# Reordering splits, copies, value products and scores inside the attention stage of a hybrid inference step

## The chip, the cores and the metric

The kernel runs on one core of a Trainium2 chip. The metric is the device time of one execution in microseconds (us); the time before is the median of three runs. A matmul works on TensorE (PE in the profile, with its weight loads as PEld), element-wise work on VectorE (DVE) and ScalarE (ACT), masks on GpSimd (POOL), and SyncE (SP) starts most transfers. Each engine takes its instructions in the order in which they were written, and waits on semaphores hold up all that is written behind them on that engine.

## What is computed

Two layers of a streaming encoder for 512 prompt tokens and 64 new tokens with 512 cached rows. Layer 0 has 8 stick-breaking heads and 8 forgetting-attention (fox) heads; layer 1 is latent attention (mla); both are followed by a mixture of experts. Cut to what the change touches, layer 0 computes for every head (head size 64):

```
z = h @ w_in                                   # q, k, v of all heads
# fox head
s = q @ k.T * 64**-0.5;  p = softmax(where(pos_k <= pos_q, s + decay, -1e30));  o = p @ v
# stick-breaking head
z = q @ k.T * 64**-0.5
log_beta = where(before, log_sigmoid(z), -1e30);  log_rest = where(before, log_sigmoid(-z), 0)
a = exp(log_beta + reverse_cumsum(log_rest) - log_rest);  o = a @ v
```

## The kernel before

Heads are taken two at a time, as eight pairs: pairs 0 to 3 stick-breaking ("sb"), pairs 4 to 7 fox. `attend` is used for layer 0 (`mla` false) and for layer 1 (`mla` true); the change keeps the order of layer 1. Each pair p is cut into ten units u (5 blocks of query rows times 2 heads). Per unit, PE computes scores (L626), ACT and DVE turn them into probabilities (`shares` L801, `cut` L1065 on POOL and `stick` L969 for sb; `decay` L1051 on POOL, `logits` L957, `exponent` L811 and `even` L982 for fox), PE transposes them (`turn` L654), ACT copies the transposed ones out of PSUM (`turn_out` L819), and after both heads of a block PE multiplies them with v (`values` L665) and DVE copies the result to `mix` (`finish` L991).

Beside the attention of pair p, PE computes the projections of pair p+1, each half of q, k and v as 24 matmuls (`project_ab`, L574; a product and its two correction products, L203 to L205). The units after which they stand are in `AB_AFTER` (L384): q0 ahead of unit 0, q1 after 0, k0 after 1, k1 after 3, the transposes of k (kt) after 4, v0 after 5, v1 after 7, the transposes of v (vt) after 8. ACT and DVE copy each out of PSUM (`copy_out`, L743 and L891), and PE's next projection into the same bank waits for that copy (`banks_free`, L569).

Further work stands between these copies:

- `split(p, par, n)` (L789, L947) splits the weights of q, k or v (n = 0, 1, 2) into a high part on ACT (L193) and a low part on DVE (L197). `splits` (L711) puts w_v of p+1 after unit 1, w_q of p+2 after unit 4, w_k of p+2 after unit 8. SP reloads the weights once they are split (`load_w`, L491).
- Two ACT copies double q for both halves of the partitions, right after q1's copy (L779); two ACT copies and two DVE subtractions split k, right after k1's copy (L784, L938).
- `split_past` splits the cached keys, after unit 0's copies on ACT and after unit 1's on DVE. SP loads the next ones when DVE's part is done (`load_past`, L501).

The order on PE in one pair (L680) is: scores of units 0 to 3; then per unit the turn, the value product of an earlier block (at u = 3, 5, 7, 9), the scores of unit u+4, the projections; at the end the value product of the last block. On each engine the order is exactly as written out in its own `pair` function; there is no planner.

Of the kernel before, what the change touches and what calls it, by code (L numbers as in the profile page):

```python
# [388 lines left out]
def attend(k, mla, m, gates=None):  # L389
# [6 lines left out]
    with ExitStack() as c:  # L396
# [83 lines left out]

        def steps_after(after, u):
            return [name for name in after if after[name] == u]

        with nc.Block() as block:
# [83 lines left out]
            def _(pe):  # L568
# [111 lines left out]
                def pair(p, par, kind, more):  # L680
# [30 lines left out]
            def splits(split, p, par, u):  # L711
# [11 lines left out]
            def first_copies(split, copy_out, gates_part):  # L723
# [5 lines left out]
                for step in copied:  # L729
                    copy_out(0, 0, step)  # L730
                    if not mla:
                        {"q1": lambda: split(0, 0, 2), "k1": lambda: split(1, 1, 0), "v1": lambda: split(1, 1, 1)}.get(step, lambda: None)()
# [3 lines left out]
            def _(act):  # L736
# [6 lines left out]
                def copy_out(p, par, step):  # L743
# [35 lines left out]
                    if step == "q1":  # L779
                        hi = q_hi[par]  # L780
                        hold(act, passed, (s["proj_act"], n), (s["q_hi_done"], 2 * p + 2))
                        copy(r32(hi[0][HD:P, :]), hi[0][0:HD, :])
                        copy(r32(hi[1][0:HD, :]), hi[1][HD:P, :]).then_inc(s["q_twice"], 1)
                    if step == "k1":  # L784
                        hold(act, passed, (s["proj_dve"], n))
                        copy(r32(k_both[par][0][0:HD, 0:T]), kT[0:HD, :]).then_inc(s["k_hi_done"], 1)
                        copy(r32(k_both[par][1][HD:P, 0:T]), kT[HD:P, :]).then_inc(s["k_hi_done"], 1)
# [41 lines left out]
                def pair(p, par, kind, more):  # L829
# [1508 lines left out]
```

## Time and profile before

| | |
|---|---|
| median of three runs | 1471.54 us (1470.74 to 1478.39) |
| the profiled execution | 1466.02 us |
| its span in the profile | 1464.2 us |
| PE busy, all of the span | 1184.6 us (81%) |
| DVE, ACT, POOL busy | 690.8, 427.9, 246.4 us |
| layer 0's attention (scores of pair 0 to values of pair 7) | 46.2 to 363.7 us |
| mixture of experts 0, attention 1, mixture 1 | behind it, to the end |

The page of the profile gives shares over the whole span, which is a mean over four stages with different limits. The stage in question is read with three views of the trace: busy time by stretches, waits, and the timeline (start us, duration us, engine, line, operation, output<-input with shapes, count, and in brackets the idle time of that engine just before and what ended it). The granted clock is TensorE's clock as a share of 2.4 GHz, so 0.5 is 1.2 GHz.

### The profile page before, as it was taken

The numbers are of one execution on the slowest core, as the hardware profiler recorded it, in microseconds if no ns is written. First come the engines' busy times: TensorE is split into PE (matmuls) and PEld (weight loads), VectorE is DVE, ScalarE is ACT, GpSimd is POOL, SyncE is SP. The second block draws the span as 40 slices with busy tenths as digits, with TensorE's granted clock in tenths as the row PEclk, the third lists the DMA queues.
The fourth block names the chain that finished last, engine by engine and source line by source line (L and its number), as shares of the span: only waits on it lengthen the run. The fifth ranks groups of instructions, "written<-read, shape, count | busy, mean of one in ns | idle before, by whom it ended". The sixth has DMA issues, their size and how long they took to land. (4 is left out here: it accounts for less than half of the span.)

```text
span 1464.2 us, 24081 instructions
## 1 busy us (share of the span) xinstructions
PE 1184.6 (81%) x8068; PEld 828.9 (57%) x8068; DVE 690.8 (47%) x1875; ACT 427.9 (29%) x967; POOL 246.4 (17%) x366
## 2 busy tenths in 40 slices
PE   7887878887994999777678699999899499878770
PEld 5777767775773555444345567676577355444330
DVE  6465655554654453212264265555565435322227
ACT  5445455544310211111121244444531021111111
POOL 1222222222012232221210000000001223221113
PEclk9899989998995999999979899999999599989995
DMA  5211222322629999999770210000042999999965
GB/s 175 68 49 43 73 104 97 105 62 111 240 87 380 368 366 371 388 370 388 272 245 14 101 51 16 29 16 16 7 157 88 381 364 362 360 378 385 390 273 194
DMA packets 63200, 290.76 MB, mean 199 GB/s; under 512 B 13744, under 2 KB 24048, under 8 KB 46208
## 3 DMA queue, kind: packets, MB, share of 16 engines
q1 hardware_dynamic: 51232, 265.90, 49.1%
q0 software_dynamic: 10560, 18.90, 4.1%
q10 hardware_dynamic: 1312, 4.72, 0.8%
q8 instruction: 56, 0.92, 0.3%
q14 instruction: 40, 0.33, 0.1%
HBM read 275.91 MB, written 29.29 MB: 208 GB/s over the span
## 5 line engine op out<-in xcount | busy, mean ns | idle before, releaser
L1809 PE MATMUL psum<-w_gu,moe_xgT 128*64 128x256 f32 x1968 | 260.5, 409 | 69.7 <-DMA w_gu<-in_w_gate_up 50.1
L1809 PEld LDWEIGHTS psum<-w_gu,moe_xgT 128*64 128x64 f32 x1968 | 153.7, 146 | 160.7 <-issue 115.6
L203 PE MATMUL psum<-x_hi,ab_w_hi 128*128 128x288 f32 x384 | 121.7, 317 | 9.8 <-issue 4.3
L1857 ACT ACTIVATE moe_silu<-psum 64x256 f32<-64x256 f32 x64 | 24.2, 378 | 337.3 <-PE psum L1809 291.6
L1882 DVE COPY moe_xgT<-psum 128x512 f32<-128x512 f32 x64 | 44.3, 692 | 164.5 <-PE psum L1799 163.6
L204 PE MATMUL psum<-x_lo,ab_w_hi 128*128 128x288 f32 x384 | 119.5, 311 | 0.0
L205 PE MATMUL psum<-x_hi,ab_w_lo 128*128 128x288 f32 x384 | 119.2, 310 | 0.0
L1756 POOL DMA_INDIRECT y_d<-mix,moe_slots x60 | 55.5, 925 | 361.9 <-DVE mix L1895 361.9
L1826 PE MATMUL psum<-w_dn,moe_hidT 128*64 128x512 f32 x352 | 85.1, 604 | 2.2 <-issue 2.2
L203 PEld LDWEIGHTS psum<-x_hi,ab_w_hi 128*128 128x128 f32 x384 | 78.7, 205 | 13.7 <-issue 13.2
L1890 DVE COPY moe_hidT<-psum 128x128 f32<-128x128 f32 x64 | 18.7, 292 | 142.3 <-PE psum L1817 140.8
L204 PEld LDWEIGHTS psum<-x_lo,ab_w_hi 128*128 128x128 f32 x384 | 78.5, 204 | 0.5
L205 PEld LDWEIGHTS psum<-x_hi,ab_w_lo 128*128 128x128 f32 x384 | 78.0, 203 | 0.0
L1862 ACT ACTIVATE mix<-psum 64x512 f32<-64x512 f32 x64 | 37.7, 589 | 134.8 <-PE psum L1826 134.8
L203 PE MATMUL psum<-mix_w_hi,mix_mix_hi 128*128 128x512 f32 (+1 forms) x160 | 65.3, 408 | 11.5 <-DVE mix_w_lo L197 11.5
L1895 DVE COPY mix<-psum 64x512 f32<-64x512 f32 x64 | 44.4, 694 | 52.4 <-PE psum L1826 52.4
L661 PE MATMUL psum<-ident,w_gu 128*128 128x128 f32 (+2 forms) x240 | 38.4, 269 | 34.4 <-issue 29.9
L816 ACT ACTIVATE mla_probs<-mla_score,mla_small 128x128 f32<-128x128 f32 (+4 forms) x80 | 48.2, 603 | 57.5 <-DVE mla_small L965 56.5
L204 PE MATMUL psum<-mix_w_lo,mix_mix_hi 128*128 128x512 f32 (+1 forms) x160 | 64.1, 401 | 0.0
L205 PE MATMUL psum<-mix_w_hi,mix_mix_lo 128*128 128x512 f32 (+1 forms) x160 | 64.0, 400 | 0.0
L1745 POOL DMA_INDIRECT mix<-x_d,moe_tokens x54 | 51.0, 944 | 61.8 <-issue 58.7
L642 PE MATMUL psum<-mla_kh,mla_q 96*128 96x128 f32 (+4 forms) x160 | 59.6, 479 | 0.9 <-DVE mla_q L913 0.9
(322 smaller groups left out, 2209.8 us busy)
## 6 DMA issues: line engine op xcount, KB each, us to landing
w_gu<-in_w_gate_up SPq DMA_DIRECT2D x54, 2048.0 KB, 35.8
w_dn<-in_w_down SPq DMA_DIRECT2D x44, 1024.0 KB, 38.0
xT<-in_w_down SPq DMA_DIRECT2D x20, 1024.0 KB, 38.5
w_gu<-in_w_gate_up SPq DMA_DIRECT2D x10, 1536.0 KB, 38.9
w_gu<-in_w_out SPq DMA_DIRECT2D x4, 2048.0 KB, 9.7
combine_ys<-y_d SPq DMA_DIRECT2D x16, 512.0 KB, 7.3
xT<-in_w_gate_up SPq DMA_DIRECT2D x10, 512.0 KB, 41.0
xT<-cum_d SPq DMA_DIRECT2D x8, 544.0 KB, 6.7
```

The source lines that it names most:

```text
L203: nc.tensor.matmul(dst, r32(ah), r32(bh), start=first, stop=False)
L204: nc.tensor.matmul(dst, r32(ah), r32(bl), start=False, stop=False)
L205: return nc.tensor.matmul(dst, r32(al), r32(bh), start=False, stop=last)
L642: last = nc.tensor.matmul(slot(u)[0:rows, 0:min(width, BANK)], q, key[:, 0:min(width, BANK)], start=True, stop=True)
L661: last = nc.tensor.transpose(bank_t[0:wide, b * rows:(b + 1) * rows], at_unit(probs, u)[0:rows, b * P:b * P + wide], k.ident[0:rows, 0:rows])
L816: nc.scalar.activation(at_unit(probs, u)[0:rows], at_unit(score, u)[0:rows], ACT.Exp, scale=-1.0, bias=small[0:rows, u % NT, 0:1], accum_o ...
L1745: pool.indirect_dma_start(out=xg[n], out_offset=None, in_=k.x_d[:, :], in_offset=bass.IndirectOffsetOnAxis(ap=idx, axis=0), bounds_check=T ...
L1756: pool.indirect_dma_start(out=k.y_d[:, :], out_offset=bass.IndirectOffsetOnAxis(ap=idx, axis=0), in_=yo[n], in_offset=None, bounds_check=2 ...
L1809: last = nc.tensor.matmul(gu(s)[h * CB:(h + 1) * CB, 0:EH], xgT[:, s, j, :], gate_up_tile(k.w_gu[n], j)[:, h * EH:(h + 1) * EH], start=(j ...
L1826: last = nc.tensor.matmul(y(s)[h * CB:(h + 1) * CB, :], hidT[:, s, j, :], w_dn[n][:, j, h * BANK:(h + 1) * BANK], start=(j == 0), stop=(j ...
L1882: nc.vector.tensor_copy(xgT[:, s, :, :].rearrange("p j q -> p (j q)"), xtr(s)).then_inc(xgT_ready, 1)
L1895: nc.vector.tensor_copy(yo[n][:, BANK:D], y(s)[CB:P, :]).then_inc(y_dve, 1)
```

## The change

All of it is in `attend`, with an effect on layer 0 alone.

- PE: `values` stands at u = 2, 4, 6, 8 (then block 4 at the end), where it stood at u = 3, 5, 7, 9. Scores of units 0 to 3 of pair p+1 stand ahead of the last value product of pair p, where they stood behind it.
- ACT and DVE: in each unit the splits stand ahead of the copies of that unit's projection (`beside` is called ahead of `copies(u)`), and at other units: w_k of p+1 ahead of q0's copy (it was after unit 8 of the pair before), the past keys at 0 (ACT) and 1 (DVE), the doubling of q at 1, w_v at 3 (ACT) and 4 (DVE), the splits of k at 5 and 6, w_q of p+2 at 7 and 8.
- Before the first pair: w_v of pair 0 is split ahead of the doubling of q; w_k of pair 1 is no longer split there.

```diff
+        values_at = range(3, UNITS, 2) if mla else range(2, UNITS, 2)
 # PE, pair
-                    for u in range(LEAD):
-                        scores(p, par, u)
+                    if mla:
+                        for u in range(LEAD):
+                            scores(p, par, u)
                     projections(-1)
                     for u in range(UNITS):
                         turn(p, u, kind)
-                        if u >= 3 and u % 2:
+                        if u in values_at:
                             values(p, par, u // 2 - 1)
                         if u + LEAD < UNITS:
                             scores(p, par, u + LEAD)
                         projections(u)
+                    if more and not mla:
+                        for u in range(LEAD):
+                            scores(p + 1, 1 - par, u)
                     values(p, par, NT - 1)
 # PE, ahead of the first pair
                     pe.wait_ge(gates.tok_e, 4)
+                    for u in range(LEAD):
+                        scores(0, 0, u)
 # ACT and DVE
-            def splits(split, p, par, u):
+            def beside(p, par, u, at, split, past, twice, keys):
                 ...
-                if u == 1 and not last(1):
+                if u == at["past"]:
+                    past(p, par)
+                if last(1):
+                    return
+                if u == at["w_k"]:
+                    split(p + 1, 1 - par, 1)
+                if u == at["twice"]:
+                    twice(p + 1, 1 - par)
+                if u == at["w_v"]:
                     split(p + 1, 1 - par, 2)
-                if u == 4 and not last(2):
+                if u == at["keys"]:
+                    keys(p + 1, 1 - par)
+                if u == at["w_q"] and not last(2):
                     split(p + 2, par, 0)
-                if u == 8 and not last(2):
-                    split(p + 2, par, 1)
 # ahead of the first pair
-                        {"q1": lambda: split(0, 0, 2), "k1": lambda: split(1, 1, 0), "v1": lambda: split(1, 1, 1)}.get(step, lambda: None)()
+                    if not mla and step == "q1":
+                        split(0, 0, 2)
+                        twice(0, 0)
+                    if not mla and step == "k1":
+                        keys(0, 0)
+                        split(1, 1, 0)
 # ACT, pair
+                    beside(p, par, -1, at, split, split_past, twice, keys)
                     copies(-1)
                     for u in range(UNITS):
                         turn_out(p, u)
                         if u + LEAD - 1 < UNITS:
                             ahead(p, u + LEAD - 1)
+                        beside(p, par, u, at, split, split_past, twice, keys)
                         copies(u)
-                        if u == 0 and not mla:
-                            split_past(p, par)
-                        splits(split, p, par, u)
+                at = {"w_k": -1, "past": 0, "twice": 1, "w_v": 3, "keys": 5, "w_q": 7}
 # DVE, pair
-                        if u >= 3 and u % 2:
+                        if u in values_at:
                             finish(p, u // 2 - 1, kind)
+                        beside(p, par, u, at, split, split_past, lambda p, par: None, keys)
                         copies(u)
-                        if u == 1 and not mla:
-                            split_past(p, par)
-                        splits(split, p, par, u)
+                at = {"w_k": -1, "past": 1, "twice": None, "w_v": 4, "keys": 6, "w_q": 8}
```

`twice` and `keys` are the two doubling copies and the splits of k, taken out of `copy_out` unchanged.

## Rows read from the trace of the kernel before

**Rows 1.** The page: busy time by engine, share of the span, instructions.

```profile
PE 1184.6 (81%) x8068; PEld 828.9 (57%) x8068; DVE 690.8 (47%) x1875; ACT 427.9 (29%) x967; POOL 246.4 (17%) x366
```

**Rows 2.** Stretches: length, PE, PEld, DVE, ACT, POOL busy, clock, DMA share, GB/s.

```profile
46.20:217.70 171.50, 142.10 (x1073) 127.50 (x1073) 103.01 (x163) 88.20 (x193) 40.82 (x80) 0.92 0.21 72
88.90:130.40 41.50, 34.14 (x269) 30.50 (x269) 25.76 (x41) 21.59 (x48) 10.30 (x20) 0.96 0.20 66
...
217.70:340.70 123.00, 103.22 (x805) 91.35 (x805) 63.24 (x187) 59.80 (x142) 26.71 (x60) 0.96 0.26 81
259.25:299.30 40.05, 32.94 (x269) 29.07 (x269) 22.05 (x63) 20.61 (x48) 8.90 (x20) 1.00 0.31 96
340.70:363.70 23.00, 16.18 (x114) 11.22 (x114) 13.33 (x49) 12.32 (x34) 9.36 (x20) 0.76 0.33 124
```

**Rows 3.** Waits of PE, 46 to 364 us: in total, times, longest.

```profile
PE psum L661 <- issue: 29.9, 32, 1.3
```

**Rows 4.** Timeline, end of pair 0: values of blocks 3 and 4.

```profile
84.97 1.09 PE L676 MATMUL psum<-ab_probsT,ab_v_all 128*64 128x128 f32 x16
...
86.42 1.23 DVE L197 TENSOR_TENSOR ab_w_lo<-w_k,ab_w_hi 128x1024 fp32r<-128x1024 f32 x1 [1.37 <-ACT ab_w_hi L193]
87.57 0.28 DVE L995 COPY mix<-psum 128x128 f32 x1
...
88.09 0.80 PE L676 MATMUL psum<-ab_probsT,ab_v_all 128*64 128x64 f32 x20 [2.02 <-DVE mix L995]
```

**Rows 5.** Timeline of pair 1, units 2 and 3.

```profile
103.31 1.06 ACT L193 ACTIVATE ab_w_hi<-w_v 128x1024 fp32r<-128x1024 f32 x1
...
104.74 0.41 PE L661 MATMUL psum<-ident,w_gu 128*128 128x128 f32 x2 [1.25 <-issue]
```

**Rows 6.** Timeline of pair 1, units 4 and 5, to v0.

```profile
110.17 1.39 ACT L741 ACTIVATE ab_k_both<-ab_kT 64x576 fp32r<-64x576 f32 x2 [3.52 <-DVE ab_kT L927]
...
112.17 0.52 PE L661 MATMUL psum<-ident,w_gu 128*128 128x128 f32 x3 [1.27 <-issue]
...
112.58 1.23 DVE L976 TENSOR_TENSOR_SCAN ab_score<-ab_bias,ab_zeros 128x512 f32<-128x512 f32 x1
...
114.06 0.69 DVE L980 TENSOR_TENSOR w_gu<-w_gu,ab_score 128x511 f32<-128x511 f32 x1 [0.26 <-DVE ab_score L976]
...
114.67 0.28 DVE L930 COPY ab_k_tok<-psum 64x128 f32<-64x128 f32 x1
...
115.05 0.37 PE L203 MATMUL psum<-x_hi,ab_w_hi 128*128 128x288 f32 x1 [1.07 <-issue]
```

**Rows 7.** Groups by shape, 46 to 364 us: busy us, mean ns, idle before.

```profile
L976 DVE TENSOR_TENSOR_SCAN ab_score<-ab_bias,ab_zeros 64x576 f32<-64x576 f32 x8 | 10.9, 1365 | 4.4 <-PE psum L205 4.4
...
L197 DVE TENSOR_TENSOR lent_k_both<-ab_kT,lent_k_both 64x576 fp32r<-64x576 f32 x8 | 6.0, 753 | 4.0 <-ACT lent_k_both L741 3.9
```

**Rows 8.** Stretches behind two pair ends, columns as in rows 2.

```profile
296.00:302.00 6.00, 4.11 (x54) 3.83 (x51) 2.28 (x8) 1.67 (x5) 1.65 (x5) 1.00 0.20 53
88.00:92.00 4.00, 3.91 (x37) 3.87 (x38) 1.43 (x5) 1.34 (x6) 1.92 (x6) 0.71 0.02 4
```

**Rows 9.** Timeline of pair 6 (fox), its beginning and its ACT copies.

```profile
299.57 0.24 DVE L1012 COPY ab_cumq<-cum_tok 128x5 f32<-128x5 f32 x2
...
303.85 0.30 PE L661 MATMUL psum<-ident,w_gu 128*128 128x128 f32 x1 [0.26 <-DVE w_gu L989]
...
308.89 1.38 ACT L741 ACTIVATE lent_q_hi<-lent_q_hi 64x576 fp32r<-64x576 f32 x2
310.29 1.27 ACT L741 ACTIVATE ab_k_both<-w_gu 64x512 fp32r<-64x512 f32 x2
```

**Rows 10.** Timeline, the last value product of the last pair.

```profile
362.36 1.33 PE L676 MATMUL psum<-ab_probsT,ab_v_all 128*64 128x64 f32 x20 [0.55 <-issue]
```

**Rows 11.** Timeline ahead of pair 0.

```profile
43.98 1.23 DVE L197 TENSOR_TENSOR ab_w_lo<-w_k,ab_w_hi 128x1024 fp32r<-128x1024 f32 x1 [0.89 <-ACT ab_w_hi L193]
```

**Rows 12.** Transfers: output<-input, queue, count, size, median us to landing.

```profile
w_v<-in_w_ab SPq DMA_DIRECT2D x8, 512.0 KB, 8.2
```

More of the change, by code:

```diff
@@ L715, in splits, with first_copies @@
                 last = lambda ahead: isinstance(p, int) and p + ahead >= PAIRS
-                if u == 1 and not last(1):
+                if u == at["past"]:
[7 more added lines that the diff above has]
+                if u == at["w_v"]:
                     split(p + 1, 1 - par, 2)
-                if u == 4 and not last(2):
+                if u == at["keys"]:
+                    keys(p + 1, 1 - par)
+                if u == at["w_q"] and not last(2):
                     split(p + 2, par, 0)
-                if u == 8 and not last(2):
-                    split(p + 2, par, 1)
-            def first_copies(split, copy_out, gates_part):
+            def first_copies(split, copy_out, twice, keys, gates_part):
                 if not mla:
@@ L730, in first_copies @@
                     copy_out(0, 0, step)
-                    if not mla:
-                        {"q1": lambda: split(0, 0, 2), "k1": lambda: split(1, 1, 0), "v1": lambda: split(1, 1, 1)}.get(step, lambda: None)()
+                    if not mla and step == "q1":
[4 more added lines that the diff above has]
+                        split(1, 1, 0)
             @block.scalar
@@ L778, in copy_out, with twice, keys @@
                         last.then_inc(s["proj_act"], 1)
[L779 to L787, printed above, removed]
+                def twice(p, par):
+                    hi = q_hi[par]
+                    hold(act, passed, (s["proj_act"], STEPS * p + 2), (s["q_hi_done"], 2 * p + 2))
+                    copy(r32(hi[0][HD:P, :]), hi[0][0:HD, :])
+                    copy(r32(hi[1][0:HD, :]), hi[1][HD:P, :]).then_inc(s["q_twice"], 1)
+                def keys(p, par):
+                    hold(act, passed, (s["proj_dve"], STEPS * p + 4))
+                    copy(r32(k_both[par][0][0:HD, 0:T]), kT[0:HD, :]).then_inc(s["k_hi_done"], 1)
+                    copy(r32(k_both[par][1][HD:P, 0:T]), kT[HD:P, :]).then_inc(s["k_hi_done"], 1)
                 def split(p, par, n):
@@ L851, in gates_part @@
                     nc.scalar.preload_act_table(ACT.Sigmoid)
-                first_copies(split, copy_out, gates_part)
+                first_copies(split, copy_out, twice, keys, gates_part)
                 if not mla:
@@ L955, in split_past, with keys @@
                     split_lo(nc, both[1][0:HD, PAST_AT:], k_past[HD:P, :], both[1][HD:P, PAST_AT:]).then_inc(s["kp_lo"], 1)
+                def keys(p, par):
+                    both = k_both[par]
+                    hold(dve, passed, (s["k_hi_done"], 2 * p + 1), (s["proj_dve"], STEPS * p + 4))
+                    split_lo(nc, both[0][HD:P, 0:T], kT[0:HD, :], both[0][0:HD, 0:T])
+                    hold(dve, passed, (s["k_hi_done"], 2 * p + 2))
+                    split_lo(nc, both[1][0:HD, 0:T], kT[HD:P, :], both[1][HD:P, 0:T]).then_inc(s["k_lo_done"], 1)
                 def logits(p, u, kind):
@@ L1017, in pair @@
                         even(p, 1)
+                    beside(p, par, -1, at, split, split_past, lambda p, par: None, keys)
                     copies(-1)
@@ L1027, in pair @@
                                 even(p, u + 2)
-                        if u >= 3 and u % 2:
+                        if u in values_at:
                             finish(p, u // 2 - 1, kind)
+                        beside(p, par, u, at, split, split_past, lambda p, par: None, keys)
                         copies(u)
-                        if u == 1 and not mla:
-                            split_past(p, par)
-                        splits(split, p, par, u)
                     finish(p, NT - 1, kind)
-                first_copies(split, copy_out, lambda: gates.sums(dve))
+                at = {"w_k": -1, "past": 1, "twice": None, "w_v": 4, "keys": 6, "w_q": 8}
+                first_copies(split, copy_out, lambda p, par: None, keys, lambda: gates.sums(dve))
                 if not mla:
```

6 lines of the change are left out of this document (removed).

## The prediction

> **What bounds the kernel now.** I began with the page: PE is busy 81% of the span, DVE 47%, ACT 29% [rows 1]. That is a mean over four stages, and the change touches one, so the next view is busy time by stretch, cut where the last value product of each pair ends [rows 2]. The four stick-breaking pairs take 171.5 us with PE busy 142.1, the first three fox pairs 123.0 us with PE busy 103.2, the last pair 23.0 us. DVE is busy 60% and ACT 51% in the first of these, so neither is full: PE either works or waits for a short chain. PE's busy time itself is not all work: pair 5 ran at full clock with 32.9 us busy, and no other pair does more work, so what lies above 33 us per pair is the clock. The reader should see two kinds of loss: idle, 29.4 us in the sb pairs and 19.8 us in the fox pairs, and clock, 142.1 - 4 x 32.8 = 10.9 us and 103.2 - 3 x 32.9 = 4.5 us (32.8 for an sb pair: pair 1's 34.1 less the 1.4 us by which its slow first projection exceeds the others).
>
> Third come the waits of PE: 29.9 us in 32 waits go to the transposes of L661, put down to nothing that the profile shows [rows 3]. The timeline says what they are: each time ACT's `turn_out` of the unit before stands behind other ACT work. In pair 1 PE waits 1.25 us behind ACT's w_v split [rows 5], 1.27 us behind the two copies of k [rows 6], and so on. Seven gaps make the 7.4 us of idle of pair 1: 0.6 at turn 2, 1.25 at turn 3, 1.27 at turn 5, 1.07 ahead of v0, 0.9 at turn 7, 0.3 at vt and 2.0 at the pair's end. The last is the clearest: `finish` of block 3 waits on DVE behind w_k's low part, though its product had long been issued, and PE waits for it with value product 4 [rows 4].
>
> **The change, part by part.** I follow one sb pair along the new order, with durations from the trace, and ask at every gap who is late now.
>
> Turn 2: the gap came from the past keys on ACT (1.27 us [rows 9]), which now run while q1 is projected; zero. Turn 3: w_v's split (1.06 us [rows 5]) leaves, and value product 0 fills 0.4 us; zero. Turn 5: the 1.39 us of k's copies [rows 6] move behind `turn_out` 5; zero, and value product 1 (0.66 us) fills as well. Turn 7: value product 2 (0.9 us) stands ahead of it; 0.1 us stays. Pair's end: w_k's split is gone from there, w_q's stands behind `finish` 3, and about 1.2 us of scores stand between turn 9 and value product 4; zero.
>
> Two gaps stay, both DVE's. Ahead of v0, PE waits for kt's copy on DVE [rows 6]. From the end of k1, PE needs turn 4, values 1, scores 8, kt, turn 5, scores 9, some 3.6 us; DVE needs k's copy 0.6, stick 6 with 1.23 + 0.26 + 0.69 = 2.2 [rows 6], finish 0.28, the low part of w_v 1.23 [rows 4] (new in this place, w_q's stood behind the copy) and kt's copy 0.28, 4.65 us. So the gap is 1.05 us, as large as now. Ahead of vt: from the end of v0, DVE has stick 8 and 9, each 1.37 + 0.26 + 0.76 = 2.4 [rows 7], finish 0.3, the low parts of k 1.5 (two of 753 ns [rows 7]) and v1's copy 0.5, 7.1 us; PE arrives after 6.9 us; with the latency 0.4 us. Idle of an sb pair: 1.05 + 0.1 + 0.4 = 1.55 us. Four pairs: 29.4 - 6.2 = 23.2 us saved.
>
> Fox pairs. Turn 0 gets worse. Its chain starts when `finish` 4 is done: cumq copies on DVE, decay on POOL, logits, exponent, even; turn 0 came 4.6 us after the last value product, with 0.26 us idle [rows 9]. The 0.96 us of scores that filled this time now stand ahead, so the gap is 1.2. Turn 3: w_k's split stands on ACT ahead of q0's copy and on DVE ahead of it and of logits 3, and the past keys stand ahead of q1's copy. From exponent 2 (4.7 us behind the last value product) ACT and DVE hand over: w_k 1.05 + 1.23 + waits, q0's copies 0.9, logits 3, exponent 3, past 1.27 [rows 9], q1's copies 0.8, DVE's part 0.9, logits 4 and exponent 4, doubling q 1.38 [rows 9], `turn_out` 2: turn 3 at 15.3 us, where PE is ready at 13.5: 1.8 us, against 1.07 now. All else goes, but for 0.4 at v0. Idle of a fox pair 3.4 us; three pairs: 19.8 - 10.2 = 9.6 us saved.
>
> Ends. Ahead of pair 0 w_k's low part (1.23 us) goes from the path of the gates' copies that the first scores wait for [rows 11]: 1.2 us. In the last pair value product 3 moves into the wait for turn 9 and takes the 0.55 us of [rows 10] away: 1.2 us in all. Before pair 0 the other moves swap work on ACT and DVE while PE is busy: nothing.
>
> Cover of what is moved. SP's loads: w_v is reloaded some 5 us later in the pair, w_k within the same stretch; each is used 20 us or more later, against a landing of 8.2 us [rows 12], so nothing. If that cover failed it would cost up to those 8.2 us once per pair. POOL has idle time throughout (41 busy of 171.5 us [rows 2]).
>
> Clock. After a 2.0 us gap the clock was at its lower level (1.2 GHz) for a part of the next 4 us, 0.71 in the mean; after a gap of 1.9 us at the end of pair 5 it stayed full, 1.00 [rows 8]. Both ends are open: none of the 15.4 us comes back, or all of it. The idle share falls from 17% to about 6%, and the one clean pair is not explained by its gaps, so I take two thirds, 10 us.
>
> The Trainium skill, "TensorE: Matmul & The Clock Gate", section "What's actually happening", says that the throttled state is the default, that activity releases it, and that the chip's observation runs free of the kernel, so the same code can meet it differently each time. The pair of stretches in [rows 8] agrees with the second half. By that rule the 10 us would be a matter of luck between 0 and 15, which moves the result between 1440 and 1425; the sum doesn't rest on it.
>
> Sum: 23.2 + 9.6 + 2.4 + 10 = 45.2 us. For waits that a walk along one pair doesn't see I take back 0.5 us for each of seven pairs, 3.5 us: 41.7. Against the profiled execution, 1466.0 - 41.7 = 1424.3 us. The median of the runs lies 5.5 us above that execution, so 1430 us. Layer 1 and both mixtures keep their order and start earlier as a whole.
>
> **Rivals.**
>
> Full gain: the clock stays full in all seven pairs and nothing unseen comes: 23.2 + 9.6 + 2.4 + 15.4 = 50.6, about 1421. For it: idle of 1.5 us per pair. Against: fox pairs keep gaps of 1.2 and 1.8 us. This is the upper part of the same mechanism.
>
> Half gain: DVE becomes the bound of the sb pairs. It has 25.8 us of work [rows 2] and some 5 us of short waits between dependent steps in a pair that is to take 34.4. If each of its three waits for a handed-over half (w_k, k, past keys) opens by 1 us, 3 us per pair return, and the clock gives nothing back: 45.2 - 21 - 10 = 14, or with half of either about 24: 1447 to 1457.
>
> Slower than before: ACT and DVE take their work in order, and each split now stands ahead of a copy that releases PE's next projection. On DVE these are w_k, past, w_v, k, w_q: 1.23 + 1.39 + 1.23 + 1.5 + 1.22 = 6.6 us per pair. It decides where these engines reach the product's copy later than the product is there; if all five are open, 6.6 eats the 5.8 us that an sb pair gains, and with a clock as in the worst pair (5.5 us lost in pair 3) the time goes to about 1478 to 1490. Against: my walk finds one of five open. The Trainium skill's "Perfetto Trace Analysis", section "Tensor Engine Instruction", calls these queues strictly first in, first out, which is what the mechanism needs; [rows 4] agree.
>
> No effect: scores ahead of the last value product wait themselves, for k's low parts, which now come at unit 6. By the walk they are done 4 us earlier. If not, the gap of 2 us stays, with others: within 0.5% only if nearly all gains fail, 1465 to 1475.
>
> **How the numbers follow.** Forecast with its upper part 0.74 (full gain 0.14 of it), half gain 0.19, no effect 0.03, slower 0.04. The likeliest gives 1430. The range reaches from the full gain, with some 5 us below it for the spread of the runs, to the middle of the half gain: 1416 to 1451. A measurement of this kernel can tell about 0.5%, 7 us, from no change: faster 0.93, same 0.03, slower 0.04.
>
> **What would show it.** In the profile after: layer 0's attention ends near 320 us; sb pairs of 34 to 35.5 us with PE busy about 33; no PE wait above 0.3 us at turns 2, 3 and 5 of sb pairs; about 1 us ahead of v0, behind `copy_out` on DVE; fox pairs of 36 to 37.5 us with waits at turn 0 and turn 3; clock above 0.96 in both. Wrong would be: DVE-bound sb pairs of 37 us or more, a w_k or keys wait ahead of k0 or of the scores, turn 0 of sb pairs waiting, or time lost behind the stage.

## The result, and the profile after

| | before | after |
|---|---|---|
| median of four runs each, us | 1471.14 (1466.49 to 1478.39) | 1415.27 (1410.59 to 1418.69) |
| the profiled execution, us | 1466.02 | 1417.82 |
| layer 0's attention, first scores to last value product | 46.20 to 363.69 | 44.54 to 309.48 |
| what lies behind it, to the span's end | 1100.5 | 1106.5 |

The changed kernel takes 0.9614 of the time before (0.9563 to 0.9665 at 95%), 56 us less. The forecast was 1430, the range 1416 to 1451: the direction and the place were right, the gain was larger, by some 15 us against the forecast and by 0.7 us past the range's edge. Medians and intervals here and below leave out executions in the chip's slower state, which matters for one kernel alone, where one execution of four took 2345 us.

The page of the kernel after, next to [rows 1]: DVE, ACT and POOL do the same work, PE has the same number of instructions and is busy 16 us less.

```profile
PE 1168.4 (83%) x8068; PEld 817.7 (58%) x8068; DVE 687.7 (49%) x1875; ACT 427.5 (30%) x967; POOL 246.4 (17%) x366
```

Stretches of the kernel after, cut at the end of each pair's last value product (columns as in [rows 2]: length, PE, PEld, DVE, ACT, POOL busy, granted clock, DMA share, GB/s). These are pairs 0, 1, 5 and the last, then the whole stage.

```profile
44.54:79.50 34.96, 32.86 (x277) 30.08 (x277) 25.11 (x40) 22.98 (x55) 10.56 (x24) 1.00 0.29 83
79.50:113.49 33.99, 31.90 (x268) 29.04 (x268) 25.20 (x41) 21.48 (x49) 9.12 (x20) 1.00 0.28 81
...
217.44:253.27 35.83, 32.35 (x270) 29.10 (x269) 21.89 (x63) 20.62 (x48) 10.05 (x20) 1.00 0.32 108
...
288.80:309.48 20.68, 13.15 (x107) 8.97 (x106) 13.22 (x49) 12.34 (x34) 9.24 (x20) 0.83 0.32 114
44.54:309.48 264.94, 238.82 (x1990) 213.68 (x1990) 178.02 (x400) 161.06 (x370) 76.97 (x160) 0.99 0.29 93
```

Against [rows 2], pair 1 went from 41.5 to 34.0 us. Its idle time fell from 7.4 to 2.1 us, and its PE busy time from 34.1 to 31.9 us although the matmuls are the same. All seven pairs with a projection now run at clock 1.00. The stage is 52.6 us shorter and starts 1.7 us earlier.

The waits of PE in the kernel after, 44 to 309 us (total, times, longest), answer [rows 3]:

```profile
PE psum L663 <- DVE w_gu L1013: 8.4, 4, 4.6
PE psum L203 <- DVE ab_k_tok L953: 6.4, 7, 1.3
PE psum L663 <- issue: 4.1, 4, 1.5
PE psum L583 <- issue: 3.1, 4, 0.8
PE psum L663 <- ACT ab_probsT L761: 2.6, 2, 1.8
PE psum L652 <- DVE cum_tok L370: 1.2, 1, 1.2
```

The 29.9 us in 32 waits at the turns have become 6.7 in 6 (4.1 in 4, and 2.6 in 2 that the view puts down to ACT), while turn 0, behind DVE, went from 4.5 to 8.4. What is left is what the walk had named: v0 behind kt's copy on DVE (L203, once in each of seven pairs), vt behind v1's place on DVE (L583, the four sb pairs) and turns 0 and 3 of the fox pairs (L663). Of the 8.4 us at turn 0, 4.6 are the last pair's, which has no projection to fill them. Here are the two waits of pair 1 and the pair's end on PE:

```profile
99.64 0.37 PE L203 MATMUL psum<-x_hi,ab_w_hi 128*128 128x288 f32 x1 [1.23 <-DVE ab_k_tok L953]
...
110.47 0.73 PE L583 MATMUL psum<-ident,ab_vT 128*128 128x128 f32 x5 [0.77 <-issue]
...
112.69 0.80 PE L678 MATMUL psum<-ab_probsT,ab_v_all 128*64 128x64 f32 x20
```

The 2.02 us ahead of value product 4 of [rows 4] are gone: `finish` of block 3 now stands ahead of w_q's low part. DVE's timeline of pair 1 shows why v0's wait stayed:

```profile
95.48 0.46 DVE L950 COPY ab_kT<-psum 128x288 f32<-128x288 f32 x1 [0.34 <-PE psum L205]
95.85 1.21 DVE L1000 TENSOR_TENSOR_SCAN ab_score<-ab_bias,ab_zeros 128x512 f32<-128x512 f32 x1
97.33 0.69 DVE L1004 TENSOR_TENSOR w_gu<-w_gu,ab_score 128x511 f32<-128x511 f32 x1 [0.26 <-DVE ab_score L1000]
97.93 0.28 DVE L1019 COPY mix<-psum 128x128 f32 x1
98.13 1.22 DVE L197 TENSOR_TENSOR ab_w_lo<-w_v,ab_w_hi 128x1024 fp32r<-128x1024 f32 x1
99.26 0.28 DVE L953 COPY ab_k_tok<-psum 64x128 f32<-64x128 f32 x1
```

It is the chain of the forecast, link by link: k's copy, stick 6, finish, w_v's low part in its new place, kt's copy, then v0 at 99.64.

### The profile page after: what moved, and what is told of

Its sections match the earlier page's. It is cut to its first block and busy times, and to the rows that moved or that the text cites. A ratio compares the mean times of both kernels' runs of the same rounds, so it can differ in the third digit from the quotient of the medians.

```text
span 1416.0 us, 24081 instructions
## 1 busy us (share of the span) xinstructions
PE 1168.4 (83%) x8068; PEld 817.7 (58%) x8068; DVE 687.7 (49%) x1875; ACT 427.5 (30%) x967; POOL 246.4 (17%) x366
## 5 line engine op out<-in xcount | busy, mean ns | idle before, releaser
L1833 PE MATMUL psum<-w_gu,moe_xgT 128*64 128x256 f32 x1968 | 263.6, 413 | 69.2 <-DMA w_gu<-in_w_gate_up 52.3
L203 PE MATMUL psum<-x_hi,ab_w_hi 128*128 128x288 f32 x384 | 116.2, 303 | 10.0 <-DVE ab_k_tok L953 9.8
L204 PE MATMUL psum<-x_lo,ab_w_hi 128*128 128x288 f32 x384 | 114.2, 297 | 0.0
L205 PE MATMUL psum<-x_hi,ab_w_lo 128*128 128x288 f32 x384 | 114.1, 297 | 0.0
L203 PEld LDWEIGHTS psum<-x_hi,ab_w_hi 128*128 128x128 f32 x384 | 72.8, 190 | 13.0 <-issue 12.3
L203 PE MATMUL psum<-mix_w_hi,mix_mix_hi 128*128 128x512 f32 (+1 forms) x160 | 65.3, 408 | 11.5 <-DVE mix_w_lo L197 11.5
L204 PEld LDWEIGHTS psum<-x_lo,ab_w_hi 128*128 128x128 f32 x384 | 72.9, 190 | 0.3
L205 PEld LDWEIGHTS psum<-x_hi,ab_w_lo 128*128 128x128 f32 x384 | 72.9, 190 | 0.0
L838 ACT ACTIVATE mla_probs<-mla_score,mla_small 128x128 f32<-128x128 f32 (+4 forms) x80 | 48.2, 603 | 57.6 <-DVE mla_small L989 56.6
L1823 PE MATMUL psum<-ident,mix 64*128 64x64 f32 x432 | 39.0, 232 | 20.1 <-DMA mix<-x_d,moe_tokens 20.1
```

What stands on the lines that cost most here:

```text
L203: nc.tensor.matmul(dst, r32(ah), r32(bh), start=first, stop=False)
L204: nc.tensor.matmul(dst, r32(ah), r32(bl), start=False, stop=False)
L205: return nc.tensor.matmul(dst, r32(al), r32(bh), start=False, stop=last)
L838: nc.scalar.activation(at_unit(probs, u)[0:rows], at_unit(score, u)[0:rows], ACT.Exp, scale=-1.0, bias=small[0:rows, u % NT, 0:1], accum_o ...
L1823: last = nc.tensor.transpose(xtr(s)[:, j * CB:(j + 1) * CB], xg[n][:, j * P:(j + 1) * P], k.ident[0:CB, 0:CB])
L1833: last = nc.tensor.matmul(gu(s)[h * CB:(h + 1) * CB, 0:EH], xgT[:, s, j, :], gate_up_tile(k.w_gu[n], j)[:, h * EH:(h + 1) * EH], start=(j ...
```

## Experiments

All runs share one measure beside the time: the length of layer 0's attention in their trace (first scores to last value product). Its order of work is all that the edits touch. The stretch behind it is the same program in every kernel and took 1099.3 to 1107.1 us in thirteen traces, in no order that follows the edits; so the stage separates effects of 2 us or so that the whole time doesn't. Finer it isn't: pair 0 ran at clock 1.00 in one and at 0.95 in another of two kernels with the same order there, which is 1.4 us. Ratios are to the kernel before, run beside; the gaps of 1.1 and 3.3 us have two executions each, that of 2.1 us five, the others four.

| kernel | median, us | ratio (95%) | stage, us | clock in stage |
|---|---|---|---|---|
| before | 1471.1 | 1 | 317.5 | 0.92 |
| after | 1415.3 | 0.961 (0.956, 0.967) | 264.9 | 0.99 |
| values at odd units | 1430.4 | 0.973 (0.969, 0.977) | 281.2 | 0.96 |
| scores behind the last values | 1418.2 | 0.965 (0.961, 0.969) | 271.4 | 0.97 |
| old order on ACT and DVE | 1444.5 | 0.981 (0.976, 0.987) | 294.5 | 0.96 |
| w_k's split back at unit 8 | 1415.0 | 0.962 (0.958, 0.966) | 266.8 | 0.98 |
| before, w_k's split moved alone | 1452.5 | 0.988 (0.985, 0.992) | 307.7 | 0.93 |
| after, gap of 1.1 us per pair | 1422.3 | 0.968 (0.964, 0.972) | 273.9 | 0.97 |
| after, gap of 2.1 us | 1432.4 | 0.975 (0.972, 0.977) | 288.6 | 0.93 |
| after, gap of 3.3 us | 1443.6 | 0.983 (0.979, 0.987) | 298.0 | 0.92 |
| after, three steps re-placed | 1405.3 | 0.957 (0.954, 0.959) | 255.4 | 0.98 |
| the same, and the first pair's | 1400.9 | 0.954 (0.951, 0.956) | 254.3 | 0.99 |
| the same, past keys earlier | 1399.7 | 0.952 (0.949, 0.956) | 255.4 | 0.98 |

### One part of the change undone

The value products back at the odd units, all else as after:

```diff
-        values_at = range(3, UNITS, 2) if mla else range(2, UNITS, 2)
+        values_at = range(3, UNITS, 2)
```

> The changed kernel, with value products (and their copies on DVE) back at units 3, 5, 7, 9 in layer 0. Layer 0's attention took 264.4 us in the changed kernel's trace. Theory 1 (what counts is whether a product fills a wait that has no other cover): only turn 7 and turn 9 lack other cover. In sb pairs turn 7 waits 0.8 us again, but vt's wait on DVE (0.77 us) shrinks by as much, so sb pairs stay at 34.1 us; fox pairs go from 35.7 to 36.4, the last pair from 20.7 to 22: stage 268 us, +3.5. Rival 2 (every value product at an even unit is worth the 0.4 to 1.1 us it lasts): +2.5 us per pair, stage 282 us.

Measured: the stage took 281.2 us, 16.3 more than after, where I had expected a small loss. It is close to the rival's 282, but not in the rival's way, which was 2.5 us in every pair. The part I had reasoned out held: from v0 to vt took 10.8 us in both. What I had not seen stands at turn 7 and at the pair's end, where value product 3 (1.09 us) now comes when nothing waits to be covered, and at turn 3 of the fox pairs, where no value product fills the time. Two rows of PE's timeline, turn 7 of an sb pair and turn 3 of pair 5:

```profile
143.57 0.63 PE L663 MATMUL psum<-ident,w_gu 128*128 128x128 f32 x4 [0.89 <-issue]
```

```profile
243.16 0.66 PE L663 MATMUL psum<-ident,w_gu 128*128 128x128 f32 x2 [2.34 <-ACT ab_probsT L761]
```

After pair 0 the sb pairs took 35.4 us (34.0 to 34.2 after); pairs 4 and 5 took 38.9 (35.7), since behind waits of 2.1 and 2.3 us the clock fell to 0.96 there and cost 1.7 us each (a wait of 2.0 us in pair 6 left it at 1.00). Pair 0 lost 3.0 us, some 1.7 of them by the clock, which fell at its first scores behind a wait (1.21 us) that the kernel after has too. The even units are thus worth some 15 us, the second largest part, 3.4 of it clock, and in the forecast they had hardly a line of their own.

The first scores of the next pair back behind the last value product:

```diff
-                    if mla:
-                        for u in range(LEAD):
-                            scores(p, par, u)
+                    for u in range(LEAD):
+                        scores(p, par, u)
 ...
-                    if more and not mla:
-                        for u in range(LEAD):
-                            scores(p + 1, 1 - par, u)
                     values(p, par, NT - 1)
```

> The changed kernel, with scores of units 0 to 3 back behind the last value product of the pair before. Theory 1: turn_out 9 (0.47 us) and latency are uncovered, a wait of 0.8 to 1.0 us ahead of value product 4, +0.9 us per sb pair; in fox pairs the wait at turn 0 (1.2 us) falls to 0.3, so they don't change: stage 268 us, +3.5, clock still full. Rival 2 (the 2 us gap of the kernel before comes back whole at each end, and the clock falls behind it): +2 us in seven pairs and 5 to 10 us of clock, stage 284 us.

Measured: 271.4 us, 6.4 more than after. PE's waits show the new one, ahead of value product 4, and it is what the scores had covered:

```profile
PE psum L678 <- ACT ab_probsT L755: 7.2, 8, 1.0
```

About half of the 6.4 us is that wait. The other half is clock, which I had expected to stay full: it was 0.95 in pair 0 and 0.96 in pair 3, and PE was busy for 6.8 us at the lower level, an estimated 3.4 us lost. The fox pairs kept their length (35.3 to 35.6): what the scores fill at the pair's end they leave open at turn 0.

The order on ACT and DVE as before, with the two changes of PE's order kept:

```diff
 # the kernel before, with PE's part of the change
+        values_at = range(3, UNITS, 2) if mla else range(2, UNITS, 2)
 # PE, pair
-                        if u >= 3 and u % 2:
+                        if u in values_at:
 # and the scores of pair p+1 ahead of values(p, par, NT - 1)
```

> The kernel before, with only PE's part of the change: value products at even units, scores ahead of the last value product; splits and copies stand where they stood. Theory 1 (the order on ACT and DVE is the larger part): turn 2 still waits 0.6, turn 3 0.8, turn 5 0.6, v0 1.07, the pair's end 0.9 behind w_k's split on ACT, together 4.2 us in place of 7.4: seven pairs at 3.1 us, and between none and half of the clock's 15 us: stage 317.5 - 22 - (0 to 8) = 288 to 296 us. Rival 2 (PE's order is the larger part): stage below 280 us.

Measured: 294.5 us, 29.6 more than after, inside the expectation. So ACT's and DVE's order is the largest part. Some 7.7 us of it are clock, in pairs 0 and 1 (15.4 us busy at the lower level). Undone one at a time, the three parts cost 29.6 + 16.3 + 6.4 = 52.3 us, and the whole change gained 52.6, so no large overlap between them shows. That the sums agree to 0.3 us is partly chance: each is a single trace, and together they hold an estimated 16 us of clock, more than half of it lost in pair 0.

### w_k's split

It moved farthest, and opposite to a worry of the forecast: past a pair's end, to stand ahead of q0's copy. First it goes back alone, from the kernel after (ahead of the first pair too, which the cut leaves out):

```diff
-                at = {"w_k": -1, ...}
+                at = {"w_k": None, ...}
 # ACT and DVE, pair
                         copies(u)
+                        if u == 8 and not mla and not (isinstance(p, int) and p + 2 >= PAIRS):
+                            split(p + 2, par, 1)
```

> The changed kernel, with w_k's split alone back behind vt's copies at unit 8, a pair earlier. Theory 1: turn_out 9 stands behind 1.05 us of ACT work again, scores cover most: a wait of 0.9 us ahead of value product 4 in seven pairs; in fox pairs ACT and DVE are free of w_k ahead of q0's copy, and turn 3's wait goes from 1.8 to 0.8, so fox pairs don't change: stage 264.4 + 4 x 0.9 + 1.2 ahead of pair 0 = 269 us, clock full. Rival 2 (w_k's split ahead of q0's copy costs nothing where it is): fox turn 3 waits as long as now, stage 272 us.

Measured: 266.8 us against 264.9, and the same time. The sb pairs lost 0.9 us each, by a wait of 0.83 ahead of value product 4, and the fox pairs won as much or more:

```profile
221.11:256.06 34.95, 32.31 (x270) 29.13 (x269) 22.13 (x64) 20.71 (x48) 9.14 (x20) 1.00 0.35 110
```

That is pair 5, 35.8 us in the kernel after. Its turn 3 doesn't wait at all any more, where it had waited 1.78 us and I had expected 0.8 to stay, so w_k's split in the chain from exponent 2 was the whole of that wait. Half of the gain is given back at turn 7 and ahead of value product 4:

```profile
234.45 0.41 PE L663 MATMUL psum<-ident,w_gu 128*128 128x128 f32 x2
...
247.07 0.63 PE L663 MATMUL psum<-ident,w_gu 128*128 128x128 f32 x4 [0.32 <-issue]
...
255.26 0.80 PE L678 MATMUL psum<-ab_probsT,ab_v_all 128*64 128x64 f32 x20 [0.64 <-ACT ab_probsT L763]
```

The first scores came 0.9 us later, and the last pair took 1.6 us more at a lower clock (0.73). With the rest of the change made, this move is worth 2 us of stage in one trace and nothing in the whole time. That the split could stand early in sb pairs and late in fox pairs wasn't run. Then it alone, from the kernel before:

```diff
-                if u == 8 and not last(2):
-                    split(p + 2, par, 1)
 # ACT and DVE, pair
+                    if not mla and more:
+                        split(p + 1, 1 - par, 1)
                     copies(-1)
```

> The kernel before, with one move: w_k's split of pair p+1 stands ahead of q0's copy, no longer behind vt's copy a pair earlier. Theory 1: block 3's finish then waits only for its own product, so the wait ahead of value product 4 falls from 2.0 to 0.6 us in six pairs, and 1.2 us go ahead of pair 0; in fox pairs turn 3 waits longer by some 0.7. Idle falls by 8 to 9 us. If the 2.0 us gap is what lets the clock fall, its 15 us come back for the larger part: stage 317.5 - 9 - (8 to 15) = 293 to 300 us. Rival 2 (the clock falls with the idle share over several gaps, not with the longest one): it keeps falling, stage 303 to 309 us.

Measured: 307.7 us, 9.8 less than before, the rival's value. The gap at the end of an sb pair fell from 2.0 to 1.1 us or less, which the theory had, but the clock that was to come back with it did not: three of the seven pairs ran at 0.96 and two at 0.88. Pair 2:

```profile
123.77:166.98 43.21, 36.90 (x270) 33.21 (x269) 25.81 (x41) 21.58 (x48) 10.30 (x20) 0.88 0.19 62
```

Inside that kernel's pairs 0 to 3 no gap is over 1.3 us. No fall of the clock stands behind a pair's end any more. In the seven pairs it falls seven times, each time at a run of waits of 0.6 to 1.3 us, two within some three us of each other. So the theory that the 2 us gaps alone cost the clock fell here, and the trace of the kernel before could have told. Of its eight falls in these pairs after the one at the first scores, three follow a pair's end and five stand at such runs of shorter waits. Here is one of these, with the four us behind it, against the end of pair 3, where the wait of 2.02 us left the clock full:

```profile
185.66 0.41 PE L661 MATMUL psum<-ident,w_gu 128*128 128x128 f32 x2 [0.58 <-issue]
...
187.78 0.41 PE L661 MATMUL psum<-ident,w_gu 128*128 128x128 f32 x2 [1.24 <-issue]
...
216.88 0.80 PE L676 MATMUL psum<-ab_probsT,ab_v_all 128*64 128x64 f32 x20 [2.02 <-DVE mix L995]
```

```profile
188.66:192.66 4.00, 4.00 (x18) 3.81 (x19) 3.36 (x6) 1.04 (x3) 2.05 (x4) 0.57 0.63 193
217.70:221.70 4.00, 4.00 (x31) 4.00 (x32) 1.40 (x10) 0.99 (x4) 2.54 (x7) 1.00 0.00 0
```

### The clock, by a gap of chosen length

I then added one gap of known length to the kernel after, at each pair's end and nowhere else. POOL, which is idle there, runs a chain of small fills once the last turn is copied out, and PE waits for it ahead of the last value product:

```diff
 # POOL, at the end of pair
+                        steps = Steps(pool, s["idling"], base=GAPN * p, passed=passed)
+                        for n in range(GAPN):
+                            steps.then(pool.memset(idle_at[:], 0.0))
+                        pool.sem_inc(s["held_up"], 1)
 # PE
+                    if more and not mla:
+                        hold(pe, passed, (s["held_up"], p + 1))
                     values(p, par, NT - 1)
```

Eight fills:

> The changed kernel, with a delay added: at the end of each of the first seven pairs PE waits, ahead of the last value product, for eight small memsets that GpSimd runs one after the other once the last turn is done, about 2.8 us, of which the scores cover 1.2. So one gap of some 1.6 to 2 us per pair, and no other gap changes. Theory 1 (the clock's gain came from the end of this gap): stage 264.9 + 7 x 1.8 = 277.5, and the clock falls in several pairs, another 5 to 12 us: 283 to 290 us, granted clock 0.93 to 0.97. Rival 2 (idle share): with 9 to 11% idle the clock stays at 1.00, stage 277 to 279 us.

Five fills:

> The changed kernel with the added delay of g1_gap_at_end cut from eight memsets to five: the gap at each pair's end is 1.2 us in place of 2.1, the idle share of an sb pair about 9%. Theory 1 (one gap of 2 us lets the clock fall, one of 1.2 doesn't): clock 1.00 in the seven pairs, stage 264.9 + 7 x 1.1 = 273 us. Rival 2 (the clock follows the idle share): 0.97 to 0.99, stage 275 to 279 us.

Twelve fills:

> The same with twelve memsets: a gap of 3.3 us, idle share about 14%. Theory 1 (each such gap costs its length and a stretch at 1.2 GHz behind it, whatever its length from 2 us on): stage 288.6 + 7 x 1.2 = 297 us, clock 0.93 to 0.95. Rival 2 (the loss grows with the idle share): clock 0.85 to 0.90, stage above 303 us.

Measured: 288.6, 273.9 and 298.0 us. The three gaps show in PE's waits (eight, five, twelve fills):

```profile
PE psum L680 <- POOLq L1106: 13.5, 7, 2.1
```

```profile
PE psum L680 <- POOLq L1106: 7.1, 7, 1.1
```

```profile
PE psum L680 <- POOLq L1106: 22.5, 7, 3.4
```

The gaps of 1.1 us cost 9.0 us for 7.1 of waits, those of 2.1 us cost 23.7 for 13.5, those of 3.3 us 33.0 for 22.5. All three are near the first theory's values. Some 1.6 us of each lie in the last pair, whose clock was 0.66 instead of 0.83. In the seven pairs the surplus over the wait is 0.2, 8.7 and 8.8 us, where 1.7 of the 8.7 were lost at the first scores and not at a gap: it comes with the step from 1.1 to 2.1 and grows little beyond. These are single traces, and that with eight fills is the slowest of its five executions, 8.5 us above their median. In the whole time the three gaps cost 10, 20 and 31 us against the kernel after by the ratios, 7, 17 and 28 by the medians. So the size of each surplus is open by a few us; that the gap of 2.1 us costs more than its wait holds either way. Pair 1 of each shows it as PE busy time, at 31.90 in the kernel after. Eight, five and twelve fills:

```profile
84.42:121.88 37.46, 33.42 (x269) 30.54 (x269) 25.18 (x41) 21.68 (x48) 10.18 (x27) 0.96 0.25 73
```

```profile
80.44:115.54 35.10, 31.98 (x268) 29.08 (x268) 25.18 (x41) 21.63 (x48) 9.67 (x25) 1.00 0.27 78
```

```profile
83.33:123.35 40.02, 34.57 (x270) 31.70 (x269) 25.18 (x41) 21.66 (x48) 10.55 (x30) 0.93 0.23 68
```

and the value product behind the gap of 1.9 us is the place where it begins, against one behind a gap of 1.0 us:

```profile
120.54 1.34 PE L680 MATMUL psum<-ab_probsT,ab_v_all 128*64 128x64 f32 x20 [1.94 <-POOLq L1106]
121.81 0.61 PE L204 MATMUL psum<-x_hi,ab_w_hi 128*128 128x288 f32 x1
122.22 0.44 PE L205 MATMUL psum<-x_lo,ab_w_hi 128*128 128x288 f32 x1
122.45 0.44 PE L206 MATMUL psum<-x_hi,ab_w_lo 128*128 128x288 f32 x1
```

```profile
114.74 0.80 PE L680 MATMUL psum<-ab_probsT,ab_v_all 128*64 128x64 f32 x20 [1.03 <-POOLq L1106]
115.71 0.37 PE L204 MATMUL psum<-x_hi,ab_w_hi 128*128 128x288 f32 x1 [0.17 <-issue]
115.92 0.29 PE L205 MATMUL psum<-x_lo,ab_w_hi 128*128 128x288 f32 x1
```

Matmuls of the projection start 0.24 us apart in the first and 0.13 in the second: the lower level (1.2 GHz) and the full one. Read at the work behind each gap, the lower level came 7 times of 7 behind 3.1 to 3.4 us and at none of six places behind 1.0 to 1.1. Between them it divides: 4 of 4 behind 1.94 to 2.10 us (the ends of pairs 0 to 3), 1 of 2 behind 1.86 (pair 4, not pair 5). The kernel before had 3 of 4 behind 2.0 us and 0 of 2 behind 1.9. The end of pair 6 decides nothing, as the last pair's wait of 4.6 us follows it: in both kernels the value product ran at full clock, and the clock fell right after it, here behind 1.08 us:

```profile
295.11 0.80 PE L680 MATMUL psum<-ab_probsT,ab_v_all 128*64 128x64 f32 x20 [1.08 <-POOLq L1106]
```

```profile
296.40:300.40 4.00, 0.00 (x0) 0.00 (x0) 1.50 (x10) 1.42 (x6) 3.08 (x9) 0.50 0.00 0
```

In pair 6 of the run with eight fills it also fell behind a wait of 1.61 us at turn 3, where 1.78 us in pair 5 of the kernel after had left it at 1.00. So from 1.6 to 2 us the same length falls out either way, as in [rows 8].

### What is left: the named waits

The waits that the kernel after keeps are those of the walk, so the same walk should say how to take them away. On ACT, the doubling of q goes one unit later; on DVE, the split of k one unit earlier; and cumq's copies of the next fox pair go ahead of the last `finish`:

```diff
-                at = {"w_k": -1, "past": 0, "twice": 1, "w_v": 3, "keys": 5, "w_q": 7}
+                at = {"w_k": -1, "past": 0, "twice": 2, "w_v": 3, "keys": 5, "w_q": 7}
 # DVE
-                at = {..., "w_v": 4, "keys": 6, "w_q": 8}
+                at = {..., "w_v": 4, "keys": 5, "w_q": 8}
+                    if kind == "fox" and more:
+                        decay_of(p + 1 - SB_PAIRS)
                     finish(p, NT - 1, kind)
```

(`decay_of` is cumq's two copies; ACT's copy of k0, which now comes ahead of the doubling, waits for ACT's copy of q1.)

> The changed kernel, with three more moves: q's doubling copies at unit 2 in place of 1 on ACT, k's low parts at unit 5 in place of 6 on DVE, and the cumq copies of the next fox pair ahead of the last finish. Theory 1: fox turn 0's wait goes (1.2 us, two or three pairs), turn 3's falls from 1.8 to 0.4, vt's in sb pairs from 0.8 to 0.1; v0's 1.2 stays. Stage 264.9 - 4 x 0.7 - 3.6 - 4.2 - 1.2 in the last pair = 253 us. Rival 2 (DVE is as full as PE, so the time reappears ahead of v0): stage 259 to 262 us.

Measured: 255.4 us, 9.5 less than after, and 10 us in the time; 253 were expected, and pair 0 lost 1.4 us by the clock (0.95) behind the wait ahead of the first scores. Pair 5, 35.83 in the kernel after:

```profile
215.47:248.78 33.31, 32.25 (x269) 29.01 (x269) 22.02 (x63) 20.27 (x48) 10.06 (x21) 1.00 0.35 116
```

Its idle time went from 3.5 to 1.1 us. In the sb pairs vt's wait is gone and v0's stayed. Next, ahead of pair 0, the split of k moves behind kt's copy, where it no longer stands ahead of v0:

```diff
-                    if not mla and step == "k1":
+                    if not mla and step == "kt":
                         keys(0, 0)
                         split(1, 1, 0)
```

> The kernel i1_tuned, with k's splits of pair 0 behind kt's copies ahead of the first pair, so that v0 doesn't wait for them and for w_q's split: its wait of 3.4 us falls to about 1 us, and the first scores start 2.4 us earlier, at 42.1 us; the stage keeps its length. Against i1_tuned 2.4 us less; if k's low parts delay the gates' scans on DVE instead, 1 us less.

Measured: v0's wait ahead of pair 0 fell from 3.41 to 0.89 us, the first scores start at 40.19 us instead of 45.17, and the median is 4.4 us lower, where 2.4 had been expected. Part of the rest is the clock: over the 4 us from the start of v0 it was 0.57 behind the wait of 3.41 us and is 1.00 now.

```profile
30.91 0.37 PE L203 MATMUL psum<-x_hi,ab_w_hi 128*128 128x288 f32 x1 [0.89 <-ACT ab_k_tok L761]
```

Last, the past keys one unit earlier on DVE in the sb pairs, against v0's wait:

```diff
-                        beside(p, par, u, at, ...)
+                        beside(p, par, u, dict(at, past=0) if kind == "sb" else at, ...)
```

> The kernel i2_tuned_start, with the past keys' low parts on DVE at unit 0 in place of 1 in sb pairs, where DVE otherwise idles ahead of q1's copy. Theory 1 (v0's wait is DVE's unbroken chain from q1's copy to kt's copy, now shorter by about 1 us): the wait ahead of v0 falls from 1.25 to 0.3 us in the four sb pairs, 3 to 3.6 us off the stage, about 1397 us in all. Rival 2 (that chain starts later than q1's copy): no change.

Measured: no change, as the rival had it (the stage's 1.1 us more are the clock of pair 0, 0.95 again). DVE's and PE's rows of pair 1 say why:

```profile
92.44 0.46 DVE L952 COPY ab_kT<-psum 128x288 f32<-128x288 f32 x1 [1.02 <-PE psum L205]
```

```profile
96.60 0.37 PE L203 MATMUL psum<-x_hi,ab_w_hi 128*128 128x288 f32 x1 [1.23 <-DVE ab_k_tok L955]
```

DVE only idled longer for k1's product; the chain to v0 starts there. What stands behind k1 has to go (w_v's low part into that idle time), which wasn't run. The version of this run is the fastest of the study, 1399.7 us, not told apart from the one before it.

## Why the forecast was right in kind and short in size

The forecast's sum stood against the profiled execution: 45.2 us in stage and start, less 3.5 in reserve, 41.7. Measured there were 54.2 us (363.69 to 309.48). Term by term:

| step of the sum | forecast | measured |
|---|---|---|
| idle time, four sb pairs | 23.2 | 20.8 |
| idle time, three fox pairs | 9.6 | 9.8 |
| start and last pair | 2.4 | 4.0 |
| clock (of 15.4 read as lost) | 10.0 | 17.8 |
| other PE busy time | 0 | 1.9 |
| reserve for unseen waits | -3.5 | 0 |
| sum | 41.7 | 54.3 |

PE's busy time in the seven pairs fell by 19.7 us, from 245.3 to 225.7. The trace of the kernel before has PE busy for 35.7 us at the lower level there, and the kernel after for none. The same matmuls go about half as fast at that level (starts 0.24 against 0.13 us apart, above), so 17.8 us of the 19.7 are the clock by this estimate and 1.9 are something else.

Four terms were too small, the clock by 7.8 us, the reserve by 3.5, the other busy time by 1.9 and the ends by 1.6. The idle time was 2.2 too large. The range was missed by 0.7 us, so any of the four would have kept the result inside; the clock is by far the largest, and it is the step that failed.

**The walk held.** An sb pair was walked at 1.55 us of idle and had 2.1: v0 1.23 (1.05 forecast), vt 0.77 (0.4), turn 7 nothing (0.1). Its sum for DVE ahead of v0 adds up to 4.6 us and not to 4.65, which makes the gap forecast there 1.0. A fox pair was walked at 3.4 and had 3.2 to 3.5: turn 0 1.20 (1.2), turn 3 1.78 (1.8), v0 0.47 (0.4), all in pair 5. No stall showed that the walk had missed, so the 3.5 us held back for such were wrong by their whole size. Both rivals against the gain (DVE the bound, a split standing ahead of a waited-for copy five times in a pair) are out: the one split that stood in the way is w_v's, as walked, and it left v0's wait at its old size.

**The clock was under-sized: 10 taken, some 17.8 came.** All seven pairs went to 1.00. Two things failed in this step: the loss was read as 15.4 us, since busy time with many stalls was taken for the work at full clock, and two thirds of it were taken where all came. I read the clock as a matter of the idle share, with a doubt from the pair of [rows 8], and looked behind two pair ends alone. Of the lower level in the seven pairs of the kernel before, some 10 us stand behind pair ends, some 20 behind runs of shorter waits inside the pairs, and 6 at the first scores. The change took away the waits of both kinds. The gap runs show that a rule by the longest gap was at hand: none of the gaps left in the sb pairs is over 1.3 us, none in the fox pairs over 1.8. It is not the whole rule, and was none for pair 0, where a wait of 1.21 us ahead of the first scores stands in eight of the traces and the clock fell behind it in four. The run with w_k's split alone had no gap over 1.3 us in its sb pairs and yet 0.96 and 0.88 in two of them, with idle shares of 15 to 17%; the run with the old order on ACT and DVE had 11 to 16% idle and 1.00 in pairs 2 to 6. Gaps of 2 us are mostly enough; they aren't needed, as two or three shorter waits close together did it too; and neither the longest gap nor the idle share of a pair settles the case between. That stays open.

The Trainium skill, "TensorE: Matmul & The Clock Gate", section "What's actually happening", says that the chip's observation of activity is not tied to the kernel's own time. The gaps of 1.86 us with different outcomes agree with it, and so does the wait of 1.21 us ahead of the first scores. The forecast's use of it, luck anywhere between 0 and 15 us, was too wide: what the kernel after had was mostly not luck, since with 1.1 us more of gap in each pair, or with w_k's split back, all seven pairs were at 1.00 as well. Luck is left for pair 0, 1.4 to 1.7 us. Of the kernel after itself one execution was traced.

**PE's busy time at full clock was taken for its work.** The forecast called 32.8 us of an sb pair the work. It was 31.9; the kernel before, with the lower level taken out, comes to 32.0 to 32.4. Of pairs at clock 1.00, one with one gap has 31.87 us busy (three steps re-placed), with two 31.90 (after), three 31.98 (five fills) or 31.76 (scores behind the last values), four 32.36 (values at odd units), six 32.78 (old order), seven 32.66 (w_k's split alone). Each row of a gap shows a longer first matmul behind it, 0.37 against 0.29 us, and the tail of the last ahead of it, both counted as busy. So a stall can cost more than its idle time, by up to 0.2 us here; the 31.76 shows that their number isn't all. Which share of the 0.9 us is this and which the kind of instruction that stands at the gap was not measured apart. With the clock's 2.4 us over the 15.4, this term's 1.9 and the 1.6 of the ends, and less the 2.2 by which the idle time gained less, the stage is 3.7 us past the full gain of 50.6: about 1417 where that rival had 1421. So the rival of the full gain is what came, with more behind it.

**Start and end.** The first scores' wait fell from 2.27 to 1.21 us and they came 1.65 us earlier (1.2 forecast). The last pair won 2.3 us (1.2): its idle time is no less, its busy time is, 16.2 to 13.2 us, as the scores that were counted there now stand in the pair ahead, and its clock went from 0.76 to 0.83. About 1.0 us of that is no gain, as pair 0 is longer by these scores.

**Behind the stage** nothing moved. The profiled execution after was 6 us longer there and so gained 48.2 of the 54.2 us; but its median lies 2.6 us below that execution, where before it lay 5.1 above. The forecast carried the 5.5 us over as if it belonged to the kernel; it belongs to the one execution that was profiled. The two together (6.0 against 5.5 + 2.6) are the last 2 us, from 1417 to 1415.

**The parts.** Of the cover that was claimed, SP's later reload of w_v cost nothing visible. That the three parts add up the forecast had assumed in silence, and the undone parts bear it out within what single traces can tell.

## What to carry to other kernels

On an in-order engine, write the work that waits for no product ahead of the copy that does, and check by a walk along one pair which copy becomes late; here every wait over 0.3 us of an sb pair was found so, and the same walk then found another 10 us. Where PE has a stretch with nothing to wait for, keep it (a value product, the next scores) for the place where the walk shows a gap: the even units were worth some 15 us for one line. In costing the clock, read the granted clock along the whole stage, see what stands ahead of each fall, and take the loss from PE's busy time at the lower level. Don't take PE's busy time with stalls, even at full clock, for its work.

## What the runs showed of the hardware

- An added gap of 1.9 to 2.1 us in a stretch where PE is otherwise busy 90% of the time put the clock at its lower level in 5 cases of 6, one of 3.1 to 3.4 us in 7 of 7, one of 1.0 to 1.1 us in none of 6. In the kernel before, gaps of 1.9 to 2.0 us did so in 3 cases of 6. Beside the gap itself the loss was 1.0 us per pair, and 1.3 for the gap of 3.1 to 3.4 us, in one trace each.
- Gaps of 1.3 us at most do not protect: with two or three of them close together the clock fell in some pairs (0.88) and not in others with the same waits.
- A wait of 1.21 us ahead of the first scores, behind the same work, let the clock fall in four of eight traces.
- The same PE work was busy 31.8 to 32.0 us with one to three gaps and 32.7 to 32.8 with six or seven, at clock 1.00.
- The same program behind the stage took 1099.3 to 1107.1 us in thirteen executions, so one profiled execution can't be read for effects under some 5 us outside the stage that was changed.
